# The first layer's input projection as seven block products per pair of units, in a two-layer hybrid diffusion step on one Trainium2 core

## What is computed

```python
for layer in range(2):
    shift, scale, gate = split(silu(cond) @ w_mod[layer] + b_mod[layer], 3)
    hm = rmsnorm(x, norm_g[layer]) * (1 + scale) + shift
    if layer == 0:                       # input 1024 channels, projection 6144
        u_a, z_a, b_b, c_b, v_b, z_b = split(hm @ fc_w_in, 6)
        y_a = real(fft over tokens and over groups of 256 channels of u_a) * silu(z_a)
        y_b = b_b * dwconv3(c_b * v_b) * silu(z_b)
        out = concat(y_a, y_b) @ fc_w_out
    else:
        out, states = ssd_mixer(hm)      # bidirectional Mamba-2
    x = x + gate * out
return rmsnorm(x, final_norm_g), states
```

## Time and profile before

| | us |
|---|---|
| median of 3 runs | 1177.57 (1176.67 to 1178.69) |
| profiled execution, its own time | 1178.75 |
| its span, first to last instruction | 1176.9 |
| PE busy | 1113.4 (95%) |
| DVE busy | 747.5 (64%) |
| ACT busy | 508.8 (43%) |
| POOL busy | 255.0 (22%) |

### The profile page before, as it was taken

How to read it: one execution, slowest core, us unless ns; L and a number is a source line. 1 busy time by engine, 2 the same in 40 slices (tenths; PEclk the granted TensorE clock), 3 DMA queues, 4 the chain that set the end, 5 groups by cost and what they waited for, 6 DMA issues and landing times.

```text
span 1176.9 us, 19282 instructions
## 1 busy us (share of the span) xinstructions
PE 1113.4 (95%) x7195; PEld 1040.3 (88%) x7195; DVE 747.5 (64%) x1277; ACT 508.8 (43%) x1024; POOL 255.0 (22%) x383
## 2 busy tenths in 40 slices
PE   5899999999999999999899999999999999879997
PEld 3799999999999988888899999999999999867785
DVE  1655434767575433647869696969696978766444
ACT  5322222121212133335565666666656666565321
POOL 1200000000000000012033443444443444443001
PEclk8899999999999999999999999999999999989999
DMA  9753122344444252214325343434343424272702
GB/s 314 247 154 108 53 89 89 108 136 152 150 136 143 72 203 84 84 36 161 82 92 137 87 134 104 130 108 130 108 125 100 129 83 132 81 261 92 287 19 90
DMA packets 177880, 148.06 MB, mean 126 GB/s; under 512 B 7004, under 2 KB 156868, under 8 KB 177428
## 3 DMA queue, kind: packets, MB, share of 16 engines
q1 hardware_dynamic: 172772, 130.08, 35.9%
q0 software_dynamic: 4608, 16.83, 4.3%
q10 hardware_dynamic: 432, 0.21, 0.1%
HBM read 134.32 MB, written 12.78 MB: 125 GB/s over the span
## 4 chain that ended last, share of the span: by engine, by line
PE 65%; DVE 14%; ACT 11%; issue 5%; DMA 3%; POOL 2%; SPq 0%; DVEq 0%; ACTq 0%; POOLq 0%
PE PS L295 27%; PE PS L491 15%; PE PS L1372 9%; DVE big L1582 3%; DVE big L1559 3%; PE PS L1358 2%; ACT big L1493 2%; ACT big L1505 2%; PE PS L1431 2%; ACT w_hi L262 1%; PE PS L741 1%; DMA big<-y_scr 1%; DMA big<-l_scr 1%; PE PS L1133 1%; DVE w_lo L268 1%
## 5 line engine op out<-in xcount | busy, mean ns | idle before, releaser
L268 DVE TENSOR_TENSOR w_lo<-raw_w,w_hi 128x1024 fp32r<-128x1024 f32 x128 | 162.2, 1269 | 87.7 <-ACT w_hi L262 86.1
L262 ACT ACTIVATE w_hi<-raw_w 128x1024 fp32r<-128x1024 f32 x128 | 134.4, 1052 | 109.8 <-PE PS L295 72.2
L295 PE MATMUL PS<-h_hi,w_hi 128*128 128x320 f32 x720 | 164.8, 310 | 0.0
L295 PE MATMUL PS<-h_lo,w_hi 128*128 128x320 f32 x720 | 164.1, 309 | 0.0
L295 PE MATMUL PS<-h_hi,w_lo 128*128 128x320 f32 x720 | 164.0, 309 | 0.0
L295 PEld LDWEIGHTS PS<-h_hi,w_hi 128*128 128x128 f32 x720 | 120.0, 188 | 3.4 <-ACT big L950 2.5
L295 PEld LDWEIGHTS PS<-h_hi,w_lo 128*128 128x128 f32 x720 | 120.4, 188 | 0.0
L295 PEld LDWEIGHTS PS<-h_lo,w_hi 128*128 128x128 f32 x720 | 120.3, 188 | 0.0
L1358 PE MATMUL PS<-h_hi,w_hi 128*128 128x320 f32 x480 | 118.2, 327 | 0.0
L1358 PE MATMUL PS<-h_hi,w_lo 128*128 128x320 f32 x480 | 109.4, 309 | 0.0
L1358 PE MATMUL PS<-h_lo,w_hi 128*128 128x320 f32 x480 | 109.2, 309 | 0.0
(11 more groups left out here) (234 smaller groups left out, 2299.1 us busy)
## 6 DMA issues: line engine op xcount, KB each, us to landing
raw_w<-in_fc_w_in_dram SPq DMA_DIRECT2D x48, 512.0 KB, 4.4
raw_w<-in_ssd_w_in_dram SPq DMA_DIRECT2D x48, 512.0 KB, 5.0
big<-l_scr SPq DMA_DIRECT2D x40, 512.0 KB, 4.5
big<-in_w_mod_dram POOLq DMA_DIRECT2D x16, 1024.0 KB, 5.4
big<-in_w_mod_dram SPq DMA_DIRECT2D x16, 512.0 KB, 8.2
raw_w<-in_fc_w_out_dram SPq DMA_DIRECT2D x16, 512.0 KB, 3.6
raw_w<-in_ssd_w_out_dram SPq DMA_DIRECT2D x16, 512.0 KB, 8.1
y_scr<-big SPq DMA_DIRECT2D x40, 128.0 KB, 1.8
```

The lines of the kernel that those rows point to most:

```text
L262: act.activation(w_hi[:, slot, :], raw_w[:, slot, :], ACT.Copy).then_inc(hi_ready, 1)
L268: dve.tensor_tensor(w_lo[:, slot, :], raw_w[:, slot, :], w_hi[:, slot, :].bitcast(F32), ALU.subtract).then_inc(lo_ready, 1)
L295: mm = pe.matmul(PS[:, 2 * pair + s, 0:HALF], w[:, slot, ws], h[:, kt, s * HALF:(s + 1) * HALF], start=(kt == 0 and n == 0), stop=(kt == K ...
```

## The change

Units 0 to 3 stay as they are. The other 44 units become 22 pairs (`PAIRS`, 2 to 23): a pair is 256 output channels, and the product of its weights (two halves of the input channels x two units) with the tokens (two halves of channels x two halves of 320) is done in the Strassen-Winograd form. There are seven products of half-size blocks, each 4 blocks x 3 = 12 matmuls of 320 columns (`part_pe`), on four PSUM banks used in the order 0, 1, 2, 3, 0, 1, 2.

- Of the seven weight blocks, three are weights as loaded, and four (T1 to T4) are sums that POOL makes, four TENSOR_TENSOR of 512 columns per pair (`weights_pool`). ACT and DVE split seven blocks of 512 columns (`part_hi`, `part_lo`) where they split two units of 1024.
- Four sums of token blocks are made and split once, at the start (`fourier_first_dve`, `s_hi_act`, `s_lo_dve`: eight DVE and four ACT instructions of 1280 columns).
- ACT copies the first product to SBUF (`s1`). DVE combines the others in seven operations of 320 columns with one operand in PSUM (`pair_dve`). ACT then applies SiLU to z in SBUF.
- The middle tap of the convolution and its scaling move from DVE to ACT (`tap_center`), the last product of the branch (line 997) from DVE to POOL (`yb_pool`). DVE multiplies c by v and b by the taps in SBUF.
- Weights are loaded in quarters of 256 KB (`quarter_loads`). The modulation is accumulated in tiles of one block (2 DVE instructions), at places given by `MOD_TILE`; 22 of the 32 tiles lie in the pairs, the last ten in the output projection (`OUT_TILES`, after the splits of steps 2, 4 and 9 to 16), and so do two of the four reductions on PE (before step 5 and after step 23).
- At the start, ACT executes a SiLU on one column first and the SiLU of the conditioning vectors amid the normalisation; the loads of the second column chunk wait for each half of the first; `split_lo` of the second unit comes after two of the first four tiles of `h_dve`.

```diff
-N_IN0 = 48
+N_PLAIN = 4
+PAIRS = range(2, 24)
+PARTS = 7
 N_OUT = 16
-OUT0 = N_IN0
 IN1 = OUT0 + N_OUT
...
+        B11, T2, B21, T3, T1, T4, B22 = range(PARTS)
+        BANK = (0, 1, 2, 3, 0, 1, 2)
+        U2, C11, U3, C22, TS, C21, C12 = range(1, 8)
...
+        def part_pe(pe, n, r):
+            pe.wait_ge(lo_ready, pair_base(n) + r + 1)
+            for kt in range(4):
+                ws = slice(kt * P, (kt + 1) * P)
+                hh, hl = token_part(r, kt)
+                for j, (w, h) in enumerate(((qhi[r], hh), (qhi[r], hl), (qlo[r], hh))):
+                    mm = pe.matmul(PS[:, BANK[r], 0:HALF], w[:, ws], h, start=(kt == 0 and j == 0), stop=(kt == 3 and j == 2))
+            mm.then_inc(unit_used, 3 if (n, r) == (23, B22) else 1)
...
+            else:
+                pe.wait_ge(combined, sums(n - 1, TS))
...
+            else:
+                pe.wait_ge(combined, sums(n - 1, C21))
+            part_pe(pe, n, T2)
+            if n > 2:
+                pe.wait_ge(combined, sums(n - 1, C12))
+            part_pe(pe, n, B21)
+            if n == 2:
...
+            pe.wait_ge(p1_copied, n - 1)
+            part_pe(pe, n, T1)
+            pe.wait_ge(combined, sums(n, U2))
+            part_pe(pe, n, T4)
+            pe.wait_ge(combined, sums(n, C11))
...
+            part_pe(pe, n, B22)
...
+        def part_hi(act, n, r):
+            if n == 2:
+                act.wait_ge(unit_used, r // 2 + 1)
+            else:
+                act.wait_ge(unit_used, pair_base(n - 1) + r + 1)
+            if r in (B11, B21, B22):
+                quarter_wait(act, n, {B11: 0, B21: 1, B22: 3}[r])
+            else:
+                act.wait_ge(w_sums, 4 * (n - 2) + {T1: 1, T2: 2, T4: 3, T3: 4}[r])
+            act.activation(qhi[r], b22_raw[n % 2] if r == B22 else qraw[r], ACT.Copy).then_inc(hi_ready, 3 if (n, r) == (23, B22) else 1)
+        def part_lo(dve, n, r):
+            dve.wait_ge(hi_ready, pair_base(n) + r + 1)
+            dve.tensor_tensor(qlo[r], b22_raw[n % 2] if r == B22 else qraw[r], qhi[r].bitcast(F32), ALU.subtract).then_inc(
+                lo_ready, 3 if (n, r) == (23, B22) else 1)
...
+        def weights_pool(pool, n):
+            quarter_wait(pool, n, 0)
+            if n == 2:
+                pool.wait_ge(lo_ready, 3)
+            else:
+                pool.wait_ge(lo_ready, pair_base(n - 1) + T1 + 1)
+            pool.tensor_tensor(qraw[T1], qraw[T3], qraw[B11], ALU.subtract).then_inc(w_sums, 1)
+            quarter_wait(pool, n, 1)
+            pool.wait_ge(w_sums, 4 * n - 7)
+            pool.tensor_tensor(qraw[T2], b22_raw[n % 2], qraw[T1], ALU.subtract).then_inc(w_sums, 1)
+            if n > 2:
+                pool.wait_ge(lo_ready, pair_base(n - 1) + T4 + 1)
+            pool.wait_ge(w_sums, 4 * n - 6)
+            pool.tensor_tensor(qraw[T4], qraw[T2], qraw[B21], ALU.subtract).then_inc(w_sums, 1)
+            pool.tensor_tensor(qraw[T3], b22_raw[n % 2], qraw[T3], ALU.subtract).then_inc(w_sums, 1)
...
+        MOD_TILE = {2: 0, 3: 2, 5: 5, 7: 8, 8: 11, 9: 12, 11: 13, 12: 14, 13: 15, 15: 16, 16: 17, 17: 18, 19: 19, 20: 20, 21: 21}
+        def pair_dve(dve, n):
...
+            dst = pair_dst(n)
+            if n in (4, 6, 8):
+                ya_dve(dve, n // 2 - 1)
+            if n < 23:
+                part_lo(dve, n + 1, B11)
+            dve.wait_ge(unit_used, base + T2 + 1)
+            dve.wait_ge(p1_copied, n - 1)
+            if n > 2:
+                dve.wait_ge(combined, sums(n - 1, C12))
+            dve.tensor_tensor(u2, PS[:, BANK[T2], 0:HALF], s1, ALU.add).then_inc(combined, 1)
+            if k == "b":
...
+            dve.tensor_tensor(dst[:, 0, H0], PS[:, BANK[B21], 0:HALF], s1, ALU.add).then_inc(combined, 1)
+            if k == "b":
+                tap_right(dve, i, 0)
+            if n in MOD_TILE and k not in ("v", "c"):
+                mod_tile_dve(dve, MOD_TILE[n])
+            dve.wait_ge(unit_used, base + T3 + 1)
+            dve.wait_ge(combined, sums(n, U2))
+            dve.tensor_tensor(u3, u2, PS[:, BANK[T3], 0:HALF], ALU.add).then_inc(combined, 1)
+            if n < 23:
+                part_lo(dve, n + 1, T2)
             else:
-                pe.wait_ge(row_copied, i)
-            for c in range(2):
+                y_split_dve(dve, 0, 0)
+            dve.wait_ge(unit_used, base + T1 + 1)
...
+            dve.tensor_tensor(dst[:, 1, H1], PS[:, BANK[T1], 0:HALF], u3, ALU.add).then_inc(combined, 1)
+            dve.tensor_tensor(u2, PS[:, BANK[T1], 0:HALF], u2, ALU.add).then_inc(combined, 1)
+            if n < 23:
+                part_lo(dve, n + 1, B21)
...
+            dve.wait_ge(unit_used, base + T4 + 1)
+            dve.tensor_tensor(dst[:, 0, H1], u3, PS[:, BANK[T4], 0:HALF], ALU.subtract).then_inc(combined, 1)
...
+            if n < 23:
+                part_lo(dve, n + 1, T3)
+                part_lo(dve, n + 1, T1)
...
+            dve.wait_ge(unit_used, base + B22 + 1)
+            dve.wait_ge(combined, sums(n, TS))
+            dve.tensor_tensor(dst[:, 1, H0], PS[:, BANK[B22], 0:HALF], u2, ALU.add).then_inc(combined, 1)
...
+            if n < 23:
+                part_lo(dve, n + 1, T4)
+                part_lo(dve, n + 1, B22)
...
+            if k == "za":
+                mod_tile_dve(dve, MOD_TILE[n] + 1)
+                mod_tile_dve(dve, MOD_TILE[n] + 2)
...
+            if n in MOD_TILE and k in ("v", "c"):
+                mod_tile_dve(dve, MOD_TILE[n])
...
+        def mod_tile_dve(dve, m):
+            c, k = m // 8, m % 8
+            dve.wait_ge(acc_step, 2 * m)
+            dve.wait_ge(modw_landed[m % 2], 16 * (m // 2 + 1))
...
+            for s in range(2):
+                dve.scalar_tensor_tensor(out=acc[:, s, :], in0=mod_w[:, m % 2, :], scalar=cond[:, s, k:k + 1],
+                                         in1=bias_rows if k == 0 else acc[:, s, :], op0=ALU.mult, op1=ALU.add).then_inc(acc_step, 1)
...
+        def mod_load(pool, m):
+            if m < 2:
+                pool.wait_ge(s_done, 8)
+            else:
+                pool.wait_ge(acc_step, 2 * m - 2)
+            c, k = m // 8, m % 8
+            src = wm_src[0][:, k, 2048:3072] if c == 0 else wm_src[1][:, k, 1024 * (c - 1):1024 * c]
+            pool.dma_start(mod_w[:, m % 2, :], src).then_inc(modw_landed[m % 2], 16)
...
+        def quarter_loads(sp, n):
+            pair = PAIR_COLS[n]
+            for q, (slot, kt0, col) in enumerate(((0, 0, pair[0]), (2, 4, pair[0]), (3, 0, pair[1]), (6, 4, pair[1]))):
...
+                elif q < 3:
+                    sp.wait_ge(lo_ready, pair_base(n - 1) + slot + 1)
...
+                sp.dma_start((b22_raw[n % 2] if q == 3 else qraw[slot]).rearrange("p (k n) -> p k n", n=P),
+                             fc_src[:, kt0:kt0 + 4, col:col + P]).then_inc(half_landed[q % 2], 16)
```

More of the change, by code:

```diff
@@ L40 @@
 UNITS = OUT1 + N_OUT
+SKIPPED = OUT0 // 4 - 1
 HEADS = 32
@@ new lines, in pair_act @@
+        def pair_act(act, n):
+            k = kind(n)
+            dst = pair_dst(n)
+            act.wait_ge(unit_used, pair_base(n) + B11 + 1)
+            if n > 2:
+                act.wait_ge(combined, sums(n - 1, C11))
+            act.activation(s1, PS[:, BANK[B11], 0:HALF], ACT.Copy).then_inc(p1_copied, 1)
+            if n < 23:
+                part_hi(act, n + 1, B11)
+            if k == "b":
+                tap_center(act, turn(n), 0)
+                tap_center(act, turn(n), 1)
+            if n == 7:
+                mod_row_act(act, 0)
+            if n == 15:
+                mod_row_act(act, 1)
+            if n < 23:
+                part_hi(act, n + 1, T2)
+                part_hi(act, n + 1, B21)
+                part_hi(act, n + 1, T3)
+                part_hi(act, n + 1, T1)
+            else:
+                y_split_act(act, 0, 0)
+                split_hi(act, OUT0, 0)
+                y_split_act(act, 0, 1)
+                split_hi(act, OUT0 + 1, 1)
+            if k in ("za", "zb"):
+                act.wait_ge(combined, sums(n, C21))
+                act.activation(dst[:, 0, :], dst[:, 0, :], ACT.Silu).then_inc(gates_done, 1)
+            if n < 23:
+                part_hi(act, n + 1, T4)
+                part_hi(act, n + 1, B22)
+            else:
+                split_hi(act, OUT0 + 2, 2)
+            if k in ("za", "zb"):
+                act.wait_ge(combined, sums(n, C12))
+                act.activation(dst[:, 1, :], dst[:, 1, :], ACT.Silu).then_inc(gates_done, 1)
+            if n == 23:
+                split_hi(act, OUT0 + 3, 3)
@@ L846, in fourier_dve, with ab_dve_ops @@
+        def ab_dve_ops(dve, i):
+            dve.wait_ge(ab_act, 4 * i + 1)
             dve.wait_ge(gd_ready, 5 * i + 2)
-            if not first:
+            if i:
                 dve.wait_ge(ld_ready, 2 * i)
@@ L892, in mod_reduce_pe @@
+        def mod_reduce_pe(pe, c, bank):
+            pe.wait_ge(acc_step, 16 * c + 16)
+            if c == 0:
+                pe.wait_ge(ya_done, 6)
+            for s in range(2):
```

(4 more changed lines are left out.)

656 lines of the change are left out of this document (393 added, 263 removed).

## The result

The changed kernel takes 1194.14 us (median of 4 runs, 1190.35 to 1196.58), the kernel before 1177.93 (4 runs, 1176.67 to 1178.69): ratio 1.0136, 95% interval 1.0122 to 1.0151. It is slower by 16 us where I forecast 7 faster, and just outside the range of 1144 to 1193. The profiled execution took 1193.74 us, its span is 1191.9.

What follows compares the result with a forecast made beforehand. PE bounds the kernel now; afterwards DVE, stopped by POOL's sums, would bound the convolution. Start -1.5, Fourier -7, convolution -2, output +3.5 make -7 us: 1170.5 us likeliest, forecast 1160 to 1181, 8-in-10 range 1144 to 1193.

Steps and rivals of the forecast that it cites:

- What bounds it, removals: First-layer turns: PE bounds them, and 84 matmuls a pair instead of 96 remove 38.7 us over 22 pairs.
- The signs that I had named for my forecast: Convolution: PE near 87% busy, DVE above 95%, splits' mean near 0.95 us, POOL's sums 1.6 or more, combinations 0.49.
- DVE's own sum: Convolution: DVE's work without POOL's turns is 172.5 us, below PE's 198; six POOL products add 8.3.
- The price of a turn: Each POOL sum stops DVE's splits, taps, products and tiles for about 1.1 us, but not its combinations.
- with 5 us of overlap in the group: Convolution: 5 us of overlap in each group c, v, b, zb, taking 4 x 5 off 246.5 to give 226.5 us.
- 1.5 for steps where DVE has to wait: Convolution: DVE's waits for PE add 1.5 us to 226.5, making 228, a gain of 2.
- the second rival: Slower: nothing overlaps with POOL's turns, convolution 246.5 us, Fourier 111.6, total 1196; chance 0.20.
- Two bounds so close give a little more than either: Fourier turns: DVE's 104.1 us beside PE's 103.3 give 105.5, a gain of 7 against 112.6.
- The start: Before the first pair: an earlier table load and a moved split gain 1.5 us, between 0 and 2.7.
- The output projection: Ten modulation tiles and two reductions move into this stage and add 3.5 us, from 2.5 to 8.
- third rival: PE's waits halve its clock for 4 us; at +1 us a pair beyond the sum, 1185, up to 1195; chance 0.13.

Runs made afterwards that it cites:

- the shifted list: The changed kernel with 64 one-column memsets put at the head of DVE's instruction list; 1186.06 us, ratio 1.0067.
- the tenth kernel: The kernel with all four sums on DVE, and 14 of the first 24 modulation tiles multiplied and summed by TensorE; 1198.75 us, ratio 1.0182.

## Why the prediction was wrong

**What bounds it, removals.** Right. The signs that I had named for my forecast came too: PE is busy for 89% of the convolution (I said 87) and DVE for 94% (above 95), the splits have a mean of 0.96, the sums of 1.6 to 1.8, the combinations of 0.48. They show the mechanism; they could not tell a gain of 2 us in this stage from a loss of 4. Without the sums, PE is the bound at 198.3 us, and the Fourier turns take 105.0 where I had worked out 103.3.

**DVE's own sum.** I had 172.5 + 8.3 us for the convolution with POOL's products; the run without sums shows 174.7. 6 us too much, on the safe side. (In the changed kernel's window lie three halves of tiles more and four sums fewer than I counted; the two cancel to within 1 us.)

**The price of a turn.** That sums stop splits, taps and tiles and not combinations was right; the Trainium skill's lock ("SBUF — State Buffer", section "SBUF: two separate sides") is what the rows show. The size was right as well: 1.1 us a sum where it meets splits.

**The step that failed: "with 5 us of overlap in the group", taken together with only "1.5 for steps where DVE has to wait".** Over the convolution I took off 20 us for overlap and added 1.5 for waits, 18.5 net. In the changed kernel DVE loses 45.3 us to the sums (219.9 - 174.7), which is 20.7 less than 60 x 1.1, but it is idle for 13.8: 6.9 net. With no load to wait for it is 12.8 less 3.6, 9.2 net. So about a third to a half of what I counted is there. Term by term the overlap is there (20.7 against 20) and the waits are the miss (13.8 against 1.5), 9.8 us of them splits that wait for a rounding, of which the run without loads has none. But the two are not apart, as that run shows: with the waits gone, the overlap is 12.8. I had laid out one group and put C12, U2, C11 and U3 between the sums; in the pair shown the trace has splits and the start of a tile there, because the four sums stand in a row of 6.4 us. They begin when I had them begin, some 3.2 us behind the split of T3 (2.9 to 4.1 over the pairs); what the layout had wrong is the places of DVE's work beside them and the waits that follow. The missing 11.6 us less the 6.1 of DVE's own sum give 5.5 of the 5.7 between 228 and 233.7; the rest is rounding. The prediction itself said that each 0.5 us of overlap a pair is 11 us. The point from which the second rival decides was an overlap below some 0.7 us a pair; the runs show 0.4 to 0.6. Its own convolution (246.5) was 13 too long, and its 1196 is near only because of the second layer's 7 us, which it did not have.

**Fourier: 105.5 forecast, 113.2 measured.** DVE's 107 us busy are near the 104.1 forecast. "Two bounds so close give a little more than either" was the false step: the first two pairs alone take 30.9 us (80.11 to 111.01) where PE needs 24.6. In them PE waits 3.52 us for U2 once, and behind that wait the granted clock is 0.50 for 3.4 us. Moving three tiles a turn behind the pair took 2.3 us off with the sums on DVE; the tiles and the engine of the sums together make 108.0.

**The start.** -1.5 forecast, +0.2 measured; in the variants the first pair starts between 78.7 and 82.1 us. That gain is not there, and I have not taken it apart.

**The output projection.** +3.5 forecast, +3.4 measured.

**The clock (third rival).** Its mechanism is here, its size is not. Behind three of PE's waits for U2 the granted clock is 0.50 for 3.4 us, which at 0.27 us a matmul in place of 0.147 is some 1.6 us of PE's work each (my estimate), 3 us of it in the convolution, against the 1 us a pair of the rival. How much of that reaches the time, where DVE is the bound, no run isolates. In the kernel with all sums on DVE there are five such stretches in the convolution, and in the tenth kernel four of 6.8 us, behind waits of 4.6 to 6 us.

**What no step and no rival had:** 7.2 us in the second layer, from the place of DVE's instructions. Without it the change would cost 8 us (1186.06, the shifted list), still slower. The runs show that the list is the cause; by what mechanism is only argued.

## What to carry to other kernels

When work is taken off the bounding engine and put on two that share an access, sum the busy time of the second with every turn at full price, and take overlap off only for operations that the trace already shows side by side; a layout by hand puts them where they would help. Here that gives 246.5 us for the convolution, 13 too many, but on the right side of the 230 before. Balance first, and then place: the same sums cost DVE 0.89 us each with DVE full and 0.5 with 16% of it free, and one tile at the wrong end of a pair cost 20 us. When a kernel's list of instructions grows, look at the stages that were not touched for idle time that ends in "issue", and shift the list before judging the change.
